# A residual of eight tiles: added by VectorE out of the accumulators, or put into them by TensorE

## The reference, cut to what matters

```python
for i in range(DEPTH):                      # two layers
    h = h + 0.5 * swiglu(rms_norm(h, ffn1_norm[i]), ffn1_w_in[i], ffn1_w_out[i])
    hn = rms_norm(h, mix_norm[i])
    m = recurrent_mixer(hn, ...) if i == 0 else spatial_gating_mixer(hn, ...)
    h = h + m
    h = h + 0.5 * swiglu(rms_norm(h, ffn2_norm[i]), ffn2_w_in[i], ffn2_w_out[i])

def spatial_gating_mixer(x, w_in, v_norm, w_s, b_s, w_out):
    u, v = split(gelu(x @ w_in), 2)
    ...                                      # sg: causal mixing of v over the tokens
    return (u * sg) @ w_out                  # w_out is 1024 x 1024
```

## Time and profile before

| | |
|---|---|
| median of 3 runs | 1448.73 us |
| the profiled execution, its time | 1448.88 us |
| the profiled execution, its span | 1447.1 us |
| TensorE busy | 1430.4 us (99%) |
| VectorE busy | 1094.8 us (76%) |
| ScalarE busy | 854.0 us (59%) |
| `sg_out` on TensorE, start of the first product to that of `in12` | 701.28 to 724.93 us |
| `rec_out` on TensorE, from the first identity product to the start of `in02` | 252.38 to 278.86 us |

### The profile page before, as it was taken

One profiled execution on the slowest core, in us unless ns is written; L12 is line 12 of the kernel. 1 busy time (PEld: TensorE's weight loads), 2 busy tenths in 40 slices (PEclk: granted clock), 3 DMA queues, 4 the chain that ended last, 5 costly groups with the idle time before them and its releaser, 6 DMA issues.

```text
span 1447.1 us, 27305 instructions
## 1 busy us (share of the span) xinstructions
PE 1430.4 (99%) x9633; PEld 1318.5 (91%) x9633; DVE 1094.8 (76%) x2031; ACT 854.0 (59%) x1559; POOL 273.1 (19%) x329
## 2 busy tenths in 40 slices
PE   8999999999999999999999999999999999999998
PEld 7888899988888888889988888999999999999998
DVE  6777679877756777667787766898878779976883
ACT  6665458766544666446566554656757555576762
POOL 1111113121102111014031113332250035121000
PEclk9999999999999999999999999999999999999999
DMA  6667754566565666565556565544344555434533
GB/s 211 197 194 211 233 180 131 179 185 202 183 188 182 192 187 197 185 197 164 159 171 200 181 188 175 165 143 125 89 127 142 164 154 154 127 101 123 147 119 118
DMA packets 247875, 241.25 MB, mean 167 GB/s; under 512 B 15456, under 2 KB 246736, under 8 KB 247784
## 3 DMA queue, kind: packets, MB, share of 16 engines
q1 hardware_dynamic: 244888, 236.73, 53.8%
q10 hardware_dynamic: 2896, 3.30, 0.8%
HBM read 238.92 MB, written 1.07 MB: 166 GB/s over the span
## 4 chain that ended last, share of the span: by engine, by line
PE 81%; DVE 11%; ACT 4%; issue 2%; DMA 1%; ACTq 0%; SPq 0%; DVEq 0%
PE bank L690 74%; DVE w_lo L1865 3%; ACT w_hi L1127 1%; DVE work L2467 1%; DVE work L2416 1%; PE bank L1010 1%; DVE work L1902 1%; PE bank L994 1%; DMA raw<-in_w_out_dram 1%; DVE y_both L1865 1%; DMA raw<-in_ffn_w_in_dram 1%; DVE work L2490 1%; PE bank L977 1%; PE bank L923 1%; ACT L1159 0%
## 5 line engine op out<-in xcount | busy, mean ns | idle before, releaser
L690 PE MATMUL bank<-x_both,w_hi 128*128 128x512 f32 (+2 forms) x3216 | 747.8, 336 | 0.9 <-DVE w_lo L1865 0.5
L1865 DVE TENSOR_TENSOR w_lo<-raw,w_hi 128x1024 fp32r<-128x1024 f32 (+1 forms) x429 | 519.4, 1234 | 203.8 <-ACT w_hi L1127 202.8
L1127 ACT CAST w_hi<-raw 128x1024 fp32r<-128x1024 f32 (+1 forms) x429 | 429.3, 1028 | 126.5 <-PE bank L690 108.2
L690 PEld LDWEIGHTS bank<-x_both,w_hi 128*128 128x128 f32 x3216 | 467.8, 189 | 3.9 <-DVE w_lo L1865 1.3
L690 PEld LDWEIGHTS bank<-x_both,w_lo 128*128 128x128 f32 x2312 | 405.8, 188 | 62.5
L690 PE MATMUL bank<-x_both,w_lo 128*128 128x256 f32 (+1 forms) x2312 | 462.2, 281 | 0.0
L690 PE MATMUL bank<-y_both,w_hi 128*128 128x512 f32 (+2 forms) x1376 | 331.5, 342 | 1.8 <-DVE w_lo L1865 1.0
L690 PEld LDWEIGHTS bank<-y_both,w_lo 128*128 128x128 f32 x1040 | 184.3, 188 | 31.3
L690 PE MATMUL bank<-y_both,w_lo 128*128 128x256 f32 (+1 forms) x1040 | 206.1, 280 | 0.0
L690 PEld LDWEIGHTS bank<-y_both,w_hi 128*128 128x128 f32 x1376 | 200.3, 189 | 2.8 <-DVE w_lo L1865 1.4
L1752 POOL TENSOR_TENSOR work<-work,rstd 128x256 f32<-128x256 f32 x88 | 67.0, 783 | 412.0 <-ACT work L1196 412.0
(11 more groups left out here) (312 smaller groups left out, 1394.9 us busy)
## 6 DMA issues: line engine op xcount, KB each, us to landing
raw<-in_ffn_w_in_dram SPq DMA_DIRECT2D x176, 512.0 KB, 4.2
raw<-in_w_in_dram SPq DMA_DIRECT2D x100, 512.0 KB, 3.6
raw<-in_ffn_w_out_dram SPq DMA_DIRECT2D x64, 512.0 KB, 4.5
raw<-in_w_out_dram SPq DMA_DIRECT2D x32, 512.0 KB, 4.2
raw<-in_ffn_w_out_dram SPq DMA_DIRECT2D x32, 384.0 KB, 3.6
raw<-in_rec_w_in_dram SPq DMA_DIRECT2D x16, 512.0 KB, 4.0
raw<-in_sg_w_in_dram SPq DMA_DIRECT2D x16, 512.0 KB, 4.3
raw<-in_rec_w_out_dram SPq DMA_DIRECT2D x8, 512.0 KB, 3.5
```

The source lines that it names most:

```text
L690: i_ = mm(accs[m][:, cols], w[:, j, m * P:(m + 1) * P], moving, start=begin and g == 0 and not residual, stop=final)
L1127: nc.scalar.copy(hi_part(U)[:, 0:n, :], raw[:, s, 0:n, :]).then_inc(hi_made, 1)
L1865: TT(lo_part(U)[:, 0:n, :], raw[:, s, 0:n, :], hi_part(U)[:, 0:n, :].bitcast(fp32), SUB).then_inc(lo_made, 1)
```

## The change

One name is added to a set:

```diff
-PE_ADDS = ("rec_out",)
+PE_ADDS = ("rec_out", "sg_out")
```

## The result

The changed kernel takes 1451.45 us (median of 15 runs), the kernel before 1448.73 us (median of 15): +2.7 us. The ratio is 1.0021, with a 95% interval of 1.0014 to 1.0028. The change makes the kernel slower; whether by more or by less than the 0.2% at which the chances were split, the interval does not say. The forecast was 1451.5 us. Four of all the runs told of here were far slower than the rest of their kernel (one of experiment 6, 2139.68 us, and three of the kernel before beside the experiments); the ratios leave them out, and without it the median of experiment 6 is 1449.40 us.

The account below looks back on a forecast made before the run. The prediction took TensorE, busy 99% of the span and without a gap around `sg_out`, to bound the kernel. Identity products 3.45 us less the seam's 0.63 gave +2.82 us, a forecast of 1451.5 us, range 1450.4 to 1452.5 us.

Parts of the forecast that it names:

- the 0.2% at which the chances were split: Whole time: bound of slower, 2.9 us above the median, at 1451.63 us; same 0.55, slower 0.42, faster 0.03.
- TensorE's gaps decide, and there is one near the change: `sg_out`: added TensorE work is paid in full unless in a wait; one wait, 0.45 us idle, at the `in12` seam.
- B: Rival on TensorE in `sg_out`: identity products' price partly covered, 3.45 down to 1.9 us; 1450.0 us, chance 0.16.
- The price, 3.45 us: TensorE in `sg_out`: eight full-precision identity products cost 1.73 + 4 x 0.43 = 3.45 us, with nothing covering them.
- The stall, 0.61 to 0.63 us back: Seam `sg_out` to `in12`: TensorE's wait for VectorE goes, giving back 0.63 us, bounds 0.45 and 0.72.
- the common point that the prediction used: Behind the seam, the first lower-part products; reaching them took 1.43 us in `sg_out` against 0.80 in `rec_out`.
- the upper of my two bounds: Seam `sg_out` to `in12`: 0.72 us given back if the seam became perfectly steady.
- ScalarE in time, with 1.0 us to spare: Third pair in `sg_out`: ScalarE's copies start at 726.13, end at 726.8 us; TensorE comes at 727.8 us.
- The shift reaches the end: Behind the seam: TensorE runs 155 us without a gap, so the +2.82 us should reach the end whole.
- A: Rival at the seam, tiles 4 and 5: ScalarE becomes late, stall of 1.4 us, 1453.1 us; chance with D 0.17.
- D: Rival: the seam stays late for another reason, nothing comes back, 1452.2 us; counted with A, together 0.17.
- C: Rival, second block: VectorE's 3.3 us relief removes later TensorE waits; 1448.4 us with half gone, 1445.3 with all; chance 0.05.

Follow-up runs that it names:

- experiment 6: Kernel before with the identity products taken out of the first mixer too, so VectorE adds `rec_out`'s tiles; 1449.64 us, ratio 1.0004.
- experiment 4: Changed kernel with each identity product of `sg_out` made twice; 1455.25 us (4 runs), ratio 1.0047 to the kernel before.
- experiment 1: Changed kernel, identity products kept, but VectorE instead of ScalarE copies `sg_out`'s finished tiles; 1451.99 us, ratio 1.0025 to the kernel before.
- experiment 2: Kernel before with ScalarE copying `sg_out`'s tiles, no identity products there and the second mixer's residual left out; 1447.35 us, ratio 0.9994.
- experiment 3: Changed kernel with each identity product of `sg_out` replaced by one ordinary reduced-type product; 1449.01 us, ratio 1.0004 to the kernel before.
- Experiment 8: Changed kernel with four unneeded copies on ScalarE ahead of the third pair's tiles in `sg_out`; 1452.11 us, ratio 1.0023 to the kernel before.
- experiment 7: Kernel before without identity products in either mixer, VectorE adding pairs two to four ahead of the weight splits in both; 1447.72 us, ratio 0.9993.
- experiment 5: Kernel before with VectorE adding the third pair's tiles of `sg_out` ahead of the weight unit's split; 1447.86 us, ratio 0.9992.

## Why the prediction was right

**TensorE's gaps decide, and there is one near the change.** Right. The chain of the changed kernel stays on TensorE through the phase, and experiment 4 shows that not a hundredth of the added time is hidden. The reading of the weight loads from the Trainium skill ("Perfetto Trace Analysis", section "Identifying the Most-Contended Engine"), applied to the stretch (34.00 of 34.00 us busy) and not to the span, led to the same, and the trace agrees; the rival that it would have supported over the whole span (B, partly covered) has nothing for it in `sg_out`.

**The price, 3.45 us.** Right: 3.42 with the stall left (experiment 1) and with it gone (26.46 - 23.04, against experiment 2), 3.45 for a second dose (experiment 4), 1.73 + 4 x 0.43 in the chain. That it is the full-precision product and not the insertion as such, which the prediction took from `rec_out` unproved, is shown by experiment 3.

**The stall, 0.61 to 0.63 us back.** Right in mechanism; the measured value is 0.61 us by itself (experiment 2). In the changed kernel the seam is perfectly steady, so to the common point that the prediction used it gave back 1.43 - 0.71 = 0.72 us (0.71 is 728.07 - 727.36), the upper of my two bounds. The sum to that point is then 3.45 - 0.72 = 2.73 us (read directly, from the start of the phase, 26.93 - 24.23 = 2.70), to the start of `in12` 2.81. I had said 2.82. The 0.09 us by which I put the gain too low (0.63 for 0.72) stood at `rec_out`'s seam in the one trace that I had; they aren't of the form, since in the changed kernel that seam takes 0.24 us too (278.82 - 278.58).

**ScalarE in time, with 1.0 us to spare.** Right: 0.99 us to the end of both copies. I had put the copies at 726.13 us; they start at 725.95, which with the phase's own offset of -0.14 us leaves 0.04 us. Experiment 8 shows the point beyond which the delay counts. Behind that, the forecast was too late: it put ScalarE's last work on tile 7 at 731.0 us, and it ends at 729.98, since on ScalarE no weight split stands between the third pair and the fourth. The error was on the safe side and touched no term of the sum.

**The shift reaches the end.** Right down to 1182 us in the trace, 2.6 us at both marks. At the end this execution shows only 2.1, and the difference of the medians is 2.7 us. That the median lies 0.05 us from the forecast is in part luck: the interval of the ratio reaches from 2.0 to 4.1 us. What holds the step up is the traces, not the medians.

**The rivals.** A's mechanism exists but needs a ScalarE 1.1 us later. D (the seam stays late for another reason) is what experiment 1 looks like, and it did not come. The price that I gave D is what experiment 1 measured (1452.0 us), with VectorE as the late one. That TensorE's busy time should grow by some 3.3 us holds where the change acts and not over the span. From the start of the phase to the mark at 1182 us (1184.67 in the changed kernel) it grew from 477.99 to 481.20 us, by 3.2. Ahead of the phase it is 0.5 us less (696.30 and 695.77 us), where the first transfers of x came later (waits of 3.6 instead of 3.0 us), and behind the mark 0.5 us less (256.08 and 255.61 us), where the products that the last output projection held up before are recorded as busy. Over the span 2.2 are left. The length of the phase is the better mark. C (VectorE's relief reaches further) has no support: the waits behind the phase, are the same 2.2, 2.0 and 0.6 us in the changed kernel, and the seam's 0.5 us is gone from the list. The wait for the weights' lower part is 1.2 instead of 1.5 us, but the 0.3 us less lie at 18.94 us, ahead of the change.

What the prediction did not see, though the rows bore on it: that in `rec_out` the same products fill a wait. I had used `rec_out` for its prices only, and asked why they are paid in full in `sg_out`, not why they might be free where they already stood. The two expectations on `rec_out` (experiments 6 and 7) were off by that.

## What to carry to other kernels

A form that is good in one phase says nothing for its twin: here it fills waits of TensorE in the first mixer and adds 3.45 us to a TensorE without any in the second. Before work is moved onto the engine that never stands idle, price the wait that it is to remove, start to start (0.61 us here), and ask whether the late engine can simply do the awaited step first; exchanging two steps in VectorE's order took away the same wait in the phase for nothing. And when a wait is taken away, look for the next one that was hidden under it: in the first mixer three different forms (all identity products, half of them, none) all end between 26.44 and 26.48 us, at the weights' lower part.

## What was not expected of the hardware

VectorE's split of a weight unit takes 1.2 us in most places and 1.76 us between the hand-overs of these phases. In experiment 5 the same split, moved behind the add, took 1.21 us, and the scaling pair of x behind it took 1.84 us instead of 0.48 and 0.66 plus waits. So the slowness goes with the time at which it happens and not with the instruction.

The traces say which times these are: a split is long when it starts while an instruction on two tiles (TENSOR_TENSOR) runs on GpSimd. In the kernel before (timeline of both engines):

```profile
722.62 0.74 POOL L1741 TENSOR_TENSOR sumsq<-sumsq,rms 128x256 f32<-128x256 f32 x1
722.68 1.76 DVE L1865 TENSOR_TENSOR w_lo<-raw,w_hi 128x1024 fp32r<-128x1024 f32 x1
```

Of the 397 splits of this size in that trace, 310 start with no such instruction of GpSimd under way, and none of them takes more than 1.23 us. The other 87 take from 1.21 to 1.79 us, longer the more GpSimd still had to do: 1.29 us with 0.21 us of it left, 1.51 with 0.43, 1.63 with 0.55, 1.79 with 0.71. The profile's spans on GpSimd are rough, but the ten other traces show the same: no split that starts without such an instruction takes more than 1.23 us. It goes the other way too: in experiment 5 the split started first, kept its 1.21 us, and GpSimd's instruction that started within it took 1.13 us instead of 0.82.

```profile
724.55 1.13 POOL L1742 TENSOR_TENSOR sumsq<-sumsq,sq 128x256 f32<-128x256 f32 x1 [0.66 <-ACT sq L1249]
```

This is read from traces and not shown by an experiment: no run here takes GpSimd away. If it holds, it bears on the stall of the kernel before. The two splits ahead of the add of tile 4 took 1.79 and 1.76 us; at 1.21 us each VectorE would have come 1.1 us earlier (an estimate from these two durations), which is more than the stall of 0.61 us.
